# Second mixer of a two-layer network: gate matmuls on two banks, norm and recurrences placed in pieces, gated halves turned inside the last blocks, output projection from k tile 8

## The reference

```python
n = rms_norm(h, mix_norm_g);  z = n @ w_in            # 2048 -> 4096: xr, gr, gu, gv of 1024 each
# recurrent group
xc = centred_depthwise_conv(xr, conv_w, conv_b)
for d in (forward, reverse):                          # RG-LRU, 8 heads of 128
    r, i = sigmoid(xc @ w_a + b_a), sigmoid(xc @ w_x + b_x)      # per head, 128 x 128
    log_a = -8 * softplus(-lam) * r;  a = exp(log_a)
    h_d = scan(h_t = a_t * h_(t-1) + sqrt(-expm1(2 * log_a)) * (i * xc))
a_out = gelu(gr) * (h_forward + h_reverse)
# spatial gating group
v = layer_norm(gelu(gv), ln_g, ln_b)
b_out = gelu(gu) * (w_s mixed over 128 positions (v) + b_s)
h = h + concat(a_out, b_out) @ w_out                  # 2048 -> 2048
h = h + peer(rms_norm(h), w_q, sub_keys, expert_u, expert_v)
```

## Time and profile before

| | |
|---|---|
| median of three runs | 3522.35 us |
| the profiled execution | 3514.93 us, span 3513.1 us |
| busy share of the span | TensorE 90%, VectorE 64%, ScalarE 36%, GpSimd 16% |
| mean granted TensorE clock | 0.985 of 2.4 GHz |
| bytes by DMA | 936.92 MB, mean 267 GB/s |
| xr blocks, from 1827 us | up to the first gate matmul at 1885 us |
| gv, gu, gr blocks | 1885 us to 2051 us |
| output projection | 2062 us to 2154 us |
| first expert gather | 2185 us |

### The profile page before, as it was taken

How to read it: one execution, slowest core, us unless ns; L and a number is a source line. 1 busy time by engine, 2 the same in 40 slices (tenths; PEclk the granted TensorE clock), 3 DMA queues, 4 the chain that set the end, 5 groups by cost and what they waited for, 6 DMA issues and landing times.

```text
span 3513.1 us, 34930 instructions
## 1 busy us (share of the span) xinstructions
PE 3151.0 (90%) x13518; PEld 2292.2 (65%) x13518; DVE 2237.5 (64%) x3468; ACT 1249.3 (36%) x1846; POOL 545.9 (16%) x533
## 2 busy tenths in 40 slices
PE   7999999999999999999999899999777767777776
PEld 6998988888877888888887778843222223222222
DVE  6776767775556777775566665757777554444444
ACT  5554555554435455554446652111111111000001
POOL 0000000000000000000000000445433334333332
PEclk9999999999999999999999999999999999999999
DMA  6554555546554555556565456999999999999998
GB/s 213 163 154 152 162 162 168 170 166 204 184 177 154 192 192 185 182 185 214 191 210 170 134 188 217 399 419 394 420 420 420 420 420 420 421 420 420 420 420 344
DMA packets 405740, 936.92 MB, mean 267 GB/s; under 512 B 16487, under 2 KB 246536, under 8 KB 339144
## 3 DMA queue, kind: packets, MB, share of 16 engines
q0 software_dynamic: 75936, 547.39, 37.8%
q1 hardware_dynamic: 328624, 386.96, 33.8%
q10 hardware_dynamic: 1016, 0.35, 0.0%
HBM read 932.54 MB, written 2.10 MB: 266 GB/s over the span
## 4 chain that ended last, share of the span: by engine, by line
PE 61%; DMA 28%; DVE 7%; POOL 2%; ACT 2%; issue 1%; POOLq 0%; ACTq 0%; SPq 0%; DVEq 0%
DMA Ub<-in_peer_u,ids 27%; PE W L1214 13%; PE W L1222 11%; PE W L1224 11%; PE W L1223 11%; PE W L1212 7%; DVE Ub L2234 4%; PE M L1274 1%; PE M L1362 1%; PE T L1362 1%; POOL Ub L2318 1%; PE W L1211 1%; DMA Vb<-in_peer_v,ids 1%; PE W L1184 0%; POOL Vb L2328 0%
## 5 line engine op out<-in xcount | busy, mean ns | idle before, releaser
L1824 DVE TENSOR_TENSOR wl<-raw,wh 128x1024 fp32r<-128x1024 f32 (+1 forms) x720 | 842.1, 1186 | 595.7 <-ACT wh L1443 593.7
L1443 ACT ACTIVATE wh<-raw 128x1024 fp32r<-128x1024 f32 (+1 forms) x720 | 729.0, 1028 | 789.5 <-PE W L1224 595.5
L2234 DVE CUSTOM_DVE_ANT_0 Ub<-Ub,xn 128x2048 f32<-128x2048 f32 x256 | 586.0, 2291 | 478.2 <-DMA Ub<-in_peer_u,ids 478.1
L1214 PE MATMUL W<-u,wh 128*128 128x512 f32 x2040 | 723.4, 398 | 0.0
L1212 PE MATMUL W<-u,wl 128*128 128x256 f32 x2176 | 602.9, 282 | 0.2 <-DVE u L1786 0.2
L1362 PE MATMUL W<-Vb,diag 128*128 128x512 f32 x928 | 431.6, 609 | 149.9 <-DMA Vb<-in_peer_v,ids 95.9
L1222 PE MATMUL W<-wh,u 128*128 128x512 f32 (+1 forms) x1280 | 490.5, 383 | 6.8 <-DVE wl L1824 4.9
L1224 PE MATMUL W<-wh,u 128*128 128x512 f32 (+1 forms) x1280 | 480.3, 375 | 0.0
L1223 PE MATMUL W<-wl,u 128*128 128x512 f32 (+1 forms) x1280 | 480.0, 375 | 0.0
L1214 PEld LDWEIGHTS W<-u,wh 128*128 128x128 f32 x2040 | 384.3, 188 | 89.0
L1362 PEld LDWEIGHTS W<-Vb,diag 128*128 128x128 f32 x928 | 169.6, 192 | 411.8 <-issue 332.0
(11 more groups left out here) (341 smaller groups left out, 3164.1 us busy)
## 6 DMA issues: line engine op xcount, KB each, us to landing
raw<-in_w_in SPq DMA_DIRECT2D x128, 1024.0 KB, 5.3
raw<-in_w_up SPq DMA_DIRECT2D x88, 1024.0 KB, 5.2
raw<-in_w_down SPq DMA_DIRECT2D x44, 1024.0 KB, 5.0
raw<-in_w_in SPq DMA_DIRECT2D x144, 256.0 KB, 3.6
raw<-in_w_out SPq DMA_DIRECT2D x32, 1024.0 KB, 5.0
raw<-in_w_proj_a SPq DMA_DIRECT2D x16, 1024.0 KB, 5.0
Wb<-in_peer_w_q SPq DMA_DIRECT2D x16, 1024.0 KB, 11.0
raw<-in_w_proj_b SPq DMA_DIRECT2D x4, 1024.0 KB, 5.0
```

The lines of the kernel that those rows point to most:

```text
L1214: i = q.matmul(o, vh, u[:, :, kk, :], start=False, stop=last)
L1443: q.activation(wh[:, s % NS, 0:b.half], r, ACT.Copy).then_inc(s_hi, 1)
L1824: q.tensor_tensor(wl[:, s % NS, 0:b.half], r, wh[:, s % NS, 0:b.half].bitcast(F32), SUB).then_inc(s_lo, 1)
L2234: q.tensor_tensor_reduce(U[:, :], U[:, :], xn[:, t, :], 1.0, 0.0, MUL, ADD, dots[t][:, k:k + 1]).then_inc(s_dot, 1)
```

## The change

The chunks of the output projection come in the order k = 8, 12, 0, 4. The planner pumps its tasks in the middle of each sub too, and may place a piece of ScalarE or VectorE whose input is ready up to 1.0 us after TensorE's clock. The read-outs of xr and gr become tasks. The gate matmuls alternate between M0 and M1; a recurrence's square and scan and the layer norm are placed piece by piece. The turns of the gated halves become part of `spatial`, on T0 and T1, and write their own buffer `u4`; `a_out` is a task of two halves. Buffers of the expert part (`kyT`, `gf`, `g2`, the first two `Vb`) move, because `u4` lies over the place of g2. The gate, scan, norm and copy instructions of the engines are the same, one call per piece.

```diff
-            for c in range(b.kt // b.kc):
-                self.chunks.append((b, c * b.kc))
+            for k0 in (8, 12, 0, 4) if b.src == "u4" else range(0, b.kt, b.kc):
+                self.chunks.append((b, k0))
                 for half in range(2):
-                    self.subs.append((b, c * b.kc + half * (b.kc // 2), len(self.chunks) - 1, half))
+                    self.subs.append((b, k0 + half * (b.kc // 2), len(self.chunks) - 1, half))
...
-                    good = good or t <= now and self.clock[engine] <= now + BACKLOG[engine]
+                    good = good or t <= now + 1.0 and self.clock[engine] <= now + BACKLOG[engine]
...
-            if b.src in ("u3", "u5"):
+            if b.src in ("u3", "u4", "u5"):
...
-            self.taken[s] = self.put("PE", b.kc // 2 * 2 * (0.35 if b.both else 0.431 if b.whole else 3 * (0.0134 + b.n / 2400)), t, "sub", s)
+            for part in range(2):
+                if part:
+                    self.pump()
+                self.taken[s] = self.put("PE", b.kc // 4 * 2 * (0.35 if b.both else 0.431 if b.whole else 3 * (0.0134 + b.n / 2400)), t,
+                                         "sub", s, part)
...
+    def out_xr(self, n, b):
+        t = yield "DVE", lambda: None if self.when("row") is None else max(self.ended(n), self.when("row"))
+        self.pair_free[n % 2] = self.put("DVE", 1.4, t, "out", n)
+        t = self.put("DVE", 0.7, 0.0)
+        yield "ACT", lambda: t
+        t = self.put("ACT", 1.0, t, "conv_start", b)
+        yield "DVE", lambda: t
+        self.done(("out", "xr", b), self.put("DVE", 2.8, t, "conv_rest", b))
+
+    def out_gr(self, n, b):
+        yield "DVE", lambda: self.ended(n)
+        self.pair_free[n % 2] = self.put("DVE", 1.4, self.ended(n), "out", n)
+        t = self.put("DVE", 0.7, 0.0)
+        yield "ACT", lambda: t
+        self.done(("out", "gr", b), self.put("ACT", 1.9, t, "gr_gelu", b))
...
     def gates(self, k):
-        t = self.ready["out", "xr", 3]
-        for q in range(4):
-            t = yield "PE", lambda: self.free(t, self.M0)
-            self.lru[k, q] = self.M0.take(1)
-            self.in_order("lru", 4 * k + q)
-            t = self.put("PE", 0.9, t, "lru_gate", k, q)
-            yield "ACT", lambda: None if k and self.when(("lru", k - 1)) is None else t
-            t = self.M0.free = self.put("ACT", 0.9, t, "lru_sigmoid", k, q)
+
+        xc = lambda: self.when(*(("out", "xr", b) for b in range(4)))
+        made = {}
+        for what, q in (("mm", 0), ("mm", 1), ("gate", 0), ("mm", 2), ("gate", 1), ("mm", 3), ("gate", 2), ("gate", 3)):
+            bank = (self.M0, self.M1)[q % 2]
+            if what == "mm":
+                t = yield "PE", lambda: None if xc() is None or k and self.when(("gates", k - 1)) is None else self.free(xc(), bank)
+                self.lru[k, q] = (bank.name, bank.take(1))
+                self.in_order("lru", 4 * k + q)
+                made[q] = self.put("PE", 0.9, t, "lru_gate", k, q)
+                if q == 3:
+                    self.done(("gates", k), made[q])
+            else:
+                t = yield "ACT", lambda: None if k and self.when(("lru", k - 1)) is None else max(made[q], self.when(("lru", k - 1)) + 2.0 if k else 0.0)
+                t = bank.free = self.put("ACT", 0.9, t, "lru_sigmoid", k, q)
         yield "ACT", lambda: t
         t = self.put("ACT", 4.5, t, "lru_decay", k)
-        yield "DVE", lambda: t
-        t = self.put("DVE", 2.5, t, "lru_square", k)
-        self.put("DVE", 1.2, t)
-        yield "ACT", lambda: t
-        t = self.put("ACT", 2.4, t, "lru_root", k)
-        yield "DVE", lambda: t
-        t = self.put("DVE", 5.2, t, "lru_scan", k)
+        for i in range(3):
+            yield "DVE", lambda: t
+            t2 = self.put("DVE", 1.2, t, "lru_square", k, i)
+            if i == 1:
+                root = t2
+        yield "ACT", lambda: root
+        t = self.put("ACT", 2.4, root, "lru_root", k)
+        for i in range(2 + k % 2):
+            yield "DVE", lambda: t
+            t = self.put("DVE", (1.2, 2.4, 1.2)[i], t, "lru_scan", k, i)
         self.done(("lru", k), t)
+
+    def gmlp(self):
+        t = yield "DVE", lambda: self.when(("out", "gv", 1))
+        t = self.put("ACT", 1.8, self.put("DVE", 0.5, t, "gmlp_stat"))
+        for i in range(2):
+            for j in range(3):
+                yield "DVE", lambda: t
+                t = self.put("DVE", 1.2, t, "gmlp_norm", i, j)
+        self.done("gmlp", t)
 
     def spatial(self):
         for i in range(2):
             for h0 in (0, 4):
-                t = yield "PE", lambda: None if self.when("ws") is None else self.free(self.ready["gmlp"], self.T1)
+                t = yield "PE", lambda: None if self.when("ws", "gmlp") is None else self.free(self.when("gmlp"), self.T1)
                 self.sgu[i, h0] = self.T1.take(1)
                 t = self.put("PE", 0.9, t, "sgu_mix", i, h0)
-                yield "DVE", lambda: self.when(("out", "gu", 1))
-                self.T1.free = self.put("DVE", 1.5, t, "sgu_out", i, h0)
+                yield "DVE", lambda: None if self.when(("out", "gu", 1)) is None else max(t, self.when(("out", "gu", 1)))
+                t = self.T1.free = self.put("DVE", 1.2, t, "sgu_out", i, h0)
+        for k in range(8, 16, 2):
+            bank = (self.T0, self.T1)[(k // 2) % 2]
+            t2 = yield "PE", lambda: self.free(t, bank)
+            self.uT[4, k // 2] = (bank.name, bank.take(2))
+            t2 = self.put("PE", 0.9, t2, "turn", 4, k)
+            yield "ACT", lambda: t2
+            bank.free = self.put("DVE", 0.7, self.put("ACT", 0.6, t2, "turn_hi", 4, k))
+            self.done(("turned", "u4", k // 2), bank.free)
+
+    def a_out(self):
+
+        for j in range(2):
+            t = yield "DVE", lambda: self.when(("lru", 2 * j + 1), ("out", "gr", 2 * j + 1))
+            t = self.put("DVE", 1.2, t, "a_gate", j)
+            t = yield "ACT", lambda: None if self.when("streamed 3") is None else max(t, self.when("streamed 3"))
+            t = self.put("ACT", 1.1, t, "a_hi", j)
+            yield "DVE", lambda: t
+            t = self.put("DVE", 1.2, t, "a_lo", j)
+            for kk in range(4 * j, 4 * j + 4, 2):
+                self.done(("turned", "u4", kk // 2), t)
...
+        self.start((2, 0), self.gmlp())
+        self.start((2, 1), self.spatial())
+        self.start((0, 2000), self.a_out())
         for b in range(2):
             self.stream(("gv", b))
-        self.add("gmlp_norm")
-        self.done("gmlp", self.put("DVE", 7.0, 0.0))
-        self.start((2, 0), self.spatial())
         for b in range(2):
             self.stream(("gu", b))
         for b in range(4):
             self.stream(("gr", b))
-        self.drain()
-        self.add("a_out")
-        self.turn(4, range(8, 16, 2))
+        self.done("streamed 3", self.clock["PE"])
...
+        u4 = at("u4", [2, 8, T], area.o, F32R)
...
-        g2_at = area.o
+        assert area.o == Z + 32768
+        Vb = [area.get("Vb0", [D])]
+        kyT = area.get("kyT", [16, P])
+        gf = at("gf", [D], area.o - 8192)
+        Vb.append(at("Vb1", [D], area.o))
...
+                if b.src == "u4" and kk >= 8:
+                    return u4[:, 0, kk - 8, :], u4[:, 1, kk - 8, :]
...
-                    first, last = kk == 0, kk == b.kt - 1
+                    first, last = s == b.first and k == 0, s == b.end - 1 and k == b.kc // 2 - 1
...
+                name, before = plan.lru[k, g]
+                e.wait_ge(s_bank[name], before)
+                q.matmul(banks[name][:, 0:T], lw[:, wi, :], xc[:, h, :], start=True, stop=True)
+                q.matmul(banks[name][:, T:2 * T], lw[:, 16 + wi, :], xc[:, h, :], start=True, stop=True).then_inc(s_lgate, 1)
...
+            def a_hi(j):
                 e.wait_ge(s_taken, last_of("u3"))
-                for j in range(2):
-                    e.wait_ge(s_hoa, j + 1)
-                    q.activation(uh[:, 4 * j:4 * j + 4, :], ho[:, 4 * j:4 * j + 4, :], ACT.Copy).then_inc(s_hoh, 1)
+                e.wait_ge(s_hoa, j + 1)
+                q.activation(uh[:, 4 * j:4 * j + 4, :], ho[:, 4 * j:4 * j + 4, :], ACT.Copy).then_inc(s_hoh, 1)
+
+            def turn_hi(ep, k):
+                name, _ = plan.uT[ep, k // 2]
+                e.wait_ge(s_gmx, 4)
+                e.wait_ge(s_uT, turned_at(ep, k))
+                q.activation(u4[:, 0, k - 8:k - 6, :], banks[name][:, :].rearrange("p (k t) -> p k t", k=2),
+                             ACT.Copy).then_inc(s_bank[name], 1)
```

More of the change, by code:

```diff
@@ L383, in out_now @@
                 self.put("DVE", 1.2, 0.0)
-        elif what == "xr":
-            self.until(lambda: self.when("row"))
-            t = self.pair_free[n % 2] = self.put("DVE", 1.4, t, "out", n)
-            self.put("DVE", 2.6, self.put("ACT", 0.9, self.put("DVE", 0.7, t)))
-        elif what == "gr":
-            t = self.pair_free[n % 2] = self.put("DVE", 1.4, t, "out", n)
```

(5 more changed lines are left out.)

168 lines of the change are left out of this document (92 added, 76 removed).

## The result

The changed kernel takes 3478.68 us (median of four runs, 3477.15 to 3479.22) against 3521.56 us for the kernel before in the same session: ratio 0.9878, 95% interval 0.9861 to 0.9895. That is 42.9 us faster, where 23.8 were forecast and the range ended at 3485. A second session (after_again) has 3481.29 against 3519.37 beside it, 38.1 us faster, so the gain is 38 to 43 us. The profiled executions differ by less: 3514.93 and 3478.45 us, 36.5 us.

| stage | before | after | change |
|---|---|---|---|
| start to first xr matmul | 1827.2 | 1815.5 | -11.6 |
| to first query-block matmul (the mixer) | 326.9 | 299.9 | -26.9 |
| to first expert gather | 31.1 | 29.4 | -1.7 |
| to last expert gather | 1293.3 | 1297.0 | +3.8 |
| to the end of the span | 34.7 | 34.7 | 0 |

What follows compares the result with a forecast made beforehand. TensorE's weight streaming bounds the kernel up to about 2172 us, then DMA's expert gathers. Terms 9.4 + 7.0 + 3.0 + 5.2 + 1.2 - 2 = 23.8 us off the median 3522.35 gave 3498.5 us, range 3485 to 3514.

Steps and rivals of the forecast that it cites:

- half-sub placement and the rule of +1.0 us: All stages with tasks, first block too: +2 us for new small waits; bounds -10.8 at best, +25 to +35 at worst.
- The base of the comparison: Saving of 23.8 us taken off the median 3522.35 us; the profiled execution, 3514.93, lay 7.4 under it.
- My bound for the clock: Second mixer: low clock around three of TensorE's waits loses 2.4 + 2.4 + 1.6 = 6.4 us.
- Turns and the order from k tile 8: Mixer's end: gated halves turned during the last blocks, projection from k tile 8; 7.8 + 1.6 of clock = 9.4 us saved.
- 32 places for eight pieces: Four gr blocks of four subs, with halves, hold the turns; rival of turns forced at stream's end: 9.4 lost, 3508.
- Norm in pieces: Mixer, wait at 1951: conversions come between the norm's pieces; 4.6 + 2.4 = 7.0 us saved, bounds 0 to 7.0.
- Gates by when xc is done: First gate, 1885: its task asks for the last convolution piece's time; 3.0 us saved, bounds 0 to 3.0.
- Two banks: Mixer's gate matmuls: fewer waits behind a sigmoid; 5.2 us saved, the middle of 0 to 10.4.
- Tail: Query block to gathers: scores 1.7 us earlier, 1.2 us taken; moved buffers 0; tail's order -2 to +6.
- The table loads: ScalarE in the mixer: up to ten added, 13 us, or 27 with the skill's drain; ScalarE not full either way.

Runs made afterwards that it cites:

- after_again: The changed kernel once more, unchanged, in a second session: 3481.29 us, against 3519.37 us for the kernel before beside it.
- b_both: The kernel before with only the planner's two loosened rules (placing in the middle of a sub, and +1.0 us): 3515.6 us, ratio 0.9993.
- a_norule: The changed kernel without the planner's +1.0 us, placing in the middle of a sub kept: 3517.5 us.
- before_again: The kernel before, unchanged, profiled again: median 3519.2 us over ten executions, 3514.5 to 3524.1.
- a_k0: The changed kernel with the output projection's chunks in the order 0, 4, 8, 12, turns where they are: 3488.2 us.
- a_onebank: The changed kernel with all gate matmuls in bank M0, each behind the sigmoids of the one ahead, the planner knowing it: 3492.8 us.
- a_rule05: The changed kernel with +0.5 us in place of +1.0 us in the planner's rule: 3508.7 us.
- a_rule2: The changed kernel with +2.0 us in place of +1.0 us in the planner's rule: 3498.9 us.
- a_norm: The changed kernel with the six steps of the layer norm placed in one go by the task: 3480.1 us.
- a_nohalf: The changed kernel without placing in the middle of a sub, the +1.0 us rule kept: 3514.5 us.
- a_second: The changed kernel with the first network's closing root mean squares on VectorE placed after the last turn of u3: 3475.3 us.

## Why the prediction was wrong

**The step that failed: "half-sub placement and the rule of +1.0 us", taken at +2 us.** It brought 11.6 us in the first block, and b_both shows that the two rules do it (10.3): 13.6 of the 19.1 us of error. I had the waits at 450 us (4.8 us) and the low clock behind them (up to 6), wrote "at best -10.8", and took the loss side because of one row of slack. The measured 10.7 by 900 us is that best case, nearly to the number. In the trace that cluster was the only stretch between 60 and 900 us where TensorE idled, so there was one thing for the rules to repair and 128 pieces that had slack. The loss side exists (a_norule, 3.7 us of new waits ahead of 445), but only with the half-subs alone. The last 1.3 us of the 11.6 are no doing of the change: they are the clock behind the same waits at 986.

**The base of the comparison.** The saving was taken off the median, as if the profiled execution before held the same stalls as the others. It held the same waits but less low clock behind them: 6.4 of the 19.1 us of error are this. In the second session, where the gain is 38.1, the whole error is 14.3. My bound for the clock, 6.4 us, stood for three waits and had nothing for those at 1885 and 1924; in before_again these cost 6.6.

**Turns and the order from k tile 8, 9.4 us.** The waits of 7.0 + 0.8 us are gone but for 1.0, the order alone is worth 6.9 to 9.5 (a_k0), and the mechanism held, but under a condition that I put aside: the turns must be placed by the end of the gr blocks. I counted 32 places for eight pieces on TensorE. a_norule, a_onebank, a_rule05 and a_rule2 keep all 32 and their turns are late, so TensorE's places are not what ran out.

**Norm in pieces, 7.0 us.** Wrong as a step (a_norm: nothing). The 4.6 us went all the same, with the norm placed as a task: the saving in the sum was right by luck.

**Gates by when xc is done, 3.0 us.** That wait is gone. In exchange the wait for the last turn of u3 grew from 0.2 to 4.6 us while the 3.3 us for the spatial weights went; b_both shows the same 4.6, and so does a_norule, while a_nohalf has 0.2: it is the doing of the half-subs.

**Two banks, 5.2 us.** Mis-sized: 11.5 to 14.1 us, above my upper bound of 10.4, since without them the cost is not the wait at the gates but late turns. The terms of the mixer add up to 24.6 us and 26.9 were measured, but this nearness is luck in part: what norm, banks and order cost when taken back (0, 11.5 to 14.1, 6.9 to 9.5) is not what the terms say, and a wait of 3.3 us that I had not counted went while one of 4.4 more came. What the read-outs of xr and gr as tasks and the moved buffers are worth was not tried.

**Tail, 1.2 us.** The key scores came 1.7 us earlier behind the query block, as worked out. The gathers took 3.8 us longer between first and last; in the runs without a starved stretch they range from 1293 to 1299. What sets that range stays open.

**The table loads** did not rise: ScalarE has 21 from the first xr matmul to the first query-block matmul of the changed kernel and 22 before, at 1.28 us. As before, the next activation starts 1.30 us after the load (1879.32 and 1880.62), with no drain to be seen. The Trainium skill's figure for the drain (ScalarE: Activation LUTs, What ACT_TABLE_LOAD costs) was not needed for any number of these runs.

By parts, us saved by the forecast and as measured between the profiles: mixer 24.6 and 26.9; first block and small waits -2 and 11.6; query block 1.2 and 1.7; gathers 0 and -3.8.

## What to carry to other kernels

When a change loosens a scheduler's rules, price it at the stalls that the trace of before still shows in the stages it reaches, and only then at the slack it uses up; and look for a deadline that two chains of side work share, since parts that each give 3 to 5 us alone (3515.6 and 3514.4 us here) can give 38 to 43 together once both chains are in time. Take a gain off the median only after asking which stalls the profiled execution drew cheaply: one repeat of the profile came out 9.1 us longer here. After such a change look at how late the last input of the next stage is. Where it is 1.0 us, as here, an edit that reorders the side work can cost 12 to 30 us (a_onebank, a_rule2, a_rule05), though others cost nothing (a_norm, a_second).

## What the runs showed of the hardware that was not expected

The same wait of TensorE, at the same place and of the same length (3.0 us at 1885, 3.45 at 1924), was followed by 2.4 GHz in one execution and by some 7 us of 1.2 GHz in another (window 1885 to 1945: clock 1.00 and 0.89). The same holds for the waits at 986, 1.6 and 0.9 us long: around them the clock is 1.00 in one execution of the changed kernel and 0.97 over 50 us in the other. The kernel before, with eleven waits of over 1 us from 60 us to its first gather, spreads over 9.6 us in ten executions (3514.5 to 3524.1); the changed kernel, with three, over 6.3 in eight of two sessions (3477.2 to 3483.4). That the number of waits sets the spread is not shown: a_nohalf, with eleven, spreads over 5.8 in ten.
